# Modulation gates as four rows of 128 with one-hot columns, in a bank that the down projection leaves alone

## The chip, the cores and the metric

The kernel runs on one core of a Trainium2 chip. The metric is the device time of one execution in microseconds, the median of several runs. TensorE (PE in the profile) multiplies, with weights loaded by its own load row (PEld); VectorE is DVE, ScalarE is ACT, GpSimd is POOL, and SyncE (SP) issues most transfers.

## The reference

The program is a chain of transformer blocks over 256 tokens of width 1024. What the change touches is small: in the second block each of two layers takes a modulation from a condition vector, and its gates scale what a mixer or a feed-forward network adds.

```python
cond = silu(c)
for i in range(2):
    mod = cond @ ada_w[i] + ada_b[i]              # 1024 -> 6 * 1024
    sh_m, sc_m, g_m, sh_f, sc_f, g_f = split(mod, 6)
    u = x * (1.0 + sc_m) + sh_m
    x = layer_norm(alpha * x + (1.0 + g_m) * mixer(u), ...)
    u = x * (1.0 + sc_f) + sh_f
    x = layer_norm(alpha * x + (1.0 + g_f) * ffn(u), ...)
```

The feed-forward networks of the first block, `0.5 * (silu(x @ wg) * (x @ wu)) @ wd` with 2816 hidden columns, don't depend on it. The kernel computes the modulation beside them.

## The kernel before, in words

The stages run one after the other: ffn0, ln0, mix0, ln1, ffn1, ln2, ffn2, ln3, mix1, ln4, ffn3, ln5, mlstm, ..., ffn4, ..., s5, ..., moe. A feed-forward pass (ffn0 to ffn3, and ffn4) streams its weights in 33 halves of 1 MB through a ring in SBUF. Halves 0 to 21 (`UP_HALVES` is 22) are the gate and up projections of six chunks of hidden columns (`NC` is 6; five of 512 and one of 256), halves 22 to 32 the down projection, two blocks of 128 hidden rows each. Each half is split into a high part (ScalarE's cast, `upper_act`, L1206) and a low part (VectorE's subtraction, `lower_dve`, L1212), and three products make up for a full float32 one: L967 and L968 (`two`) with the high weights, then L1000 (up) or L1113 (down) with the low weights, for which PE waits until VectorE has made them. Four banks of PSUM (of 8, 512 float32 each) hold a chunk's gate and up sums for two tiles of 128 tokens; the down projection accumulates into banks 4 to 7. Chunk 4 uses banks 4 to 7 and chunk 5 banks 0 to 3.

The modulation is 24 pieces of 512 values, six in each of the passes ffn0 to ffn3. For a piece:

- GpSimd loads 2 MB of `ada_w` in two parts (`load_ada`, L1380), each when VectorE has finished with the part before.
- VectorE multiplies and sums over eight blocks of rows into `ada_acc`, 128 x 512 (`ada`, L1348 and L1350, 16 instructions); what is left is a sum over the 128 partitions.
- PE makes that sum (`mod(c)`, L1134 to L1147) in plain float32. For shift and scale pieces it makes columns (L1146). For gate pieces it makes one row of 512: a column of ones against `ada_acc` (L1142), and then a one-hot column against the eight rows of biases in `ada_gb` (L1143) to add the bias.
- VectorE finishes it (`mod_out`, L1357 to L1371): L1366 adds 1.0 to the row and writes it to a row in SBUF, `gate_row` on partition 0 of `lnp[:, 2]`, two places in turn. `mod_ready` counts the finished pieces.
- GpSimd stores a gate row to `gate_dram` (L1395); from ln6 on the rows are read back to all partitions.

The gate pieces are the last two of each pass, c = 4 and c = 5, eight in all. Their place is written out by hand in `MOD_LATE` (L189): piece 4 after half 21, piece 5 after half 23. Piece 4 is written to bank 5 (`r.banks(c, 0)[1]`), which half 22 is to overwrite, so before half 22 PE waits for `mod_ready` of piece 4 (L1163). VectorE's order around it, in `ffn_dve`: at i = 21 the low part of half 23, `mod_out` of piece 4, the product `hidden(5)` (L1281), and the two parts of `ada` for piece 5; at i = 22 the low part of half 24; at i = 23 that of half 25 and `lower_h(5)` (L1289); at i = 24 that of half 26 and `mod_out` of piece 5. At the end of a pass PE waits for `mod_ready` of all its pieces (L1195).

The biases come by four loads in `mix_params_sp` (L576), which SP issues after half 5 of ffn0, ahead of the constants and the loads of the halves that follow.

Of the kernel before, what the change touches and what calls it, by code (L numbers as in the profile page):

```python
# [21 lines left out]
P = 128  # L22
# [163 lines left out]

UP_HALVES = 4 * NC - 2

MOD_LATE = {UP_HALVES - 1: NC - 2, UP_HALVES + 1: NC - 1}  # L189

FFN_HALVES = UP_HALVES + FT // 2

# [18 lines left out]
def program(nc, A, out, const_at, stages, ctx):  # L211
# [35 lines left out]
    qkv_w = sb("qkv_w", [P, 3, ML_T, QKV_BLOCK])  # L247
    gate_w = sb("gate_w", [P, 3 * ML_T, 2 * ML_HEADS])
    gate_b = sb("gate_b", [P, 2 * ML_HEADS])
    ada_gb = sb("ada_gb", [8, CHUNK])  # L250
    over = sb("over", [1, 1], mybir.dt.int32)
    router = sb("router", [P, KD, EXPERTS])
    mod_col = sb("mod_col", [P, DEPTH, 6, KD])
# [41 lines left out]
    half_landed = [sem(f"half_landed{i}") for i in range(SLOTS - 1)]  # L295
    ring_freed = [sem(f"ring_freed{i}") for i in range(SLOTS + 1)]
    x_landed, consts_landed, params_landed = sem("x_landed"), sem("consts_landed"), sem("params_landed")
    params_clear = sem("params_clear")
    mix_params_landed, second_params_landed = sem("mix_params_landed"), sem("second_params_landed")
    param_rows = sem("param_rows")  # L300
    param_cols = sem("param_cols")
# [266 lines left out]
    def mix_params_sp(sp):  # L568

        def load(dst, src):  # L570
            load_param(sp, mix_params_landed, NMIX, dst, src)

        ada_b = A["ada_b_2"].rearrange("l (v r n) -> l v r n", v=6, n=CHUNK)
        for l in range(DEPTH):
            for w in range(2):
                load(ada_gb[4 * l + 2 * w:4 * l + 2 * w + 2, :], ada_b[l, 2 + 3 * w])  # L576
        load(consts[:, P:], A["consts"][:, P:])
        sp.wait_ge(params_clear, 2)
        for i in range(2):
            half = slice(i * HD, (i + 1) * HD)  # L580
            load(w2bd[half, :, half], A["cmp_w2"].rearrange("l v i o -> i (l v) o"))
            load(poolbd[half, :, half], A["pool_w"].rearrange("l (t h) i o -> h i (l t) o", h=2)[i])
        load(gla_wa2[:, :, :], A["gla_wa2"].rearrange("l r n -> r l n"))
        for l in range(DEPTH):
            load(gla_norm[:, l, :], A["gla_norm_g"][l].partition_broadcast(P))
# [24 lines left out]
        pool.memset(poolbd[:, :, :], 0.0).then_inc(params_clear, 1)  # L610

    def start_dve(dve):
        dve.memset(eps[:, 0:1], 4.0 * LN_EPS)
        dve.memset(eps[:, 1:2], LN_EPS)
        dve.memset(eps[:, 3:4], np.pi / 2)
        dve.memset(eps[:, 4:5], ROUND)
        dve.memset(eps[:, 2:3], RMS_EPS).then_inc(param_rows, 1)
# [251 lines left out]
    expert_gate = late_gate[:, :, 1:]  # L869
    route = cv.take(NT, 128)  # L870
    y_low_at = cv.at
    gate_row = lnp[0:1, 2, :].rearrange("p (a n) -> p a n", a=2)
    xh = z_r[:, :, :].rearrange("p t (k n) -> p t k n", k=KD)
    upper = [ring_r[:, 3, 0:HALF], ring_r[:, 3, HALF:], tail_r[:, :]]
    cv = Carve(of=arena_r)
# [61 lines left out]
    def ffn_sp(sp, key, wg, wu, wd, e=None):  # L937
        for i in range(FFN_HALVES):
            kind, c, j = half_of(i)
            if kind == "d":  # L940
                src = rows(wd)[:, c:c + 2, :]
            else:
                c0, w = CHUNKS[c]
                k = slice(j * KD // 2, (j + 1) * KD // 2) if c < NC - 1 else slice(0, KD)
                src = rows(wg if kind == "g" else wu)[:, k, c0:c0 + w]
            load_half(sp, PN[key, i], src, e)
            if (key, i) == (0, 3):
                columns_sp(sp)
            if (key, i) == (0, 5):
                mix_params_sp(sp)  # L950
            if (key, i) == (1, 5):
                second_params_sp(sp)

    def ffn_pe(pe, r):
        key, e, tiles = r.key, r.e, r.tiles
# [177 lines left out]
        def mod(c):  # L1133

            l, a = divmod(r.n * NC + c, 12)
            v, part = divmod(a, 2)
            dst = r.banks(c, 0)[1]
            pe.wait_ge(ada_ready, 2 * (r.n * NC + c + 1))
            pe.wait_ge(mix_params_landed, NMIX[0])
            if v in (2, 5):  # L1140
                row = 4 * l + 2 * (v // 3) + part
                pe.matmul(dst[0:1, :], ones[:, 0:1], ada_acc[:, :], start=True, stop=False)  # L1142
                pe.matmul(dst[0:1, :], ident[0:8, row:row + 1], ada_gb[:, :], start=False, stop=True).then_inc(mod_done, 1)  # L1143
            else:
                for f in range(4):
                    mm = pe.matmul(dst[:, f:f + 1], ada_acc[:, f * P:(f + 1) * P], ones[:, 0:1], start=True, stop=True)  # L1146
# [3 lines left out]
        for i in range(FFN_HALVES):  # L1150
# [8 lines left out]
            if i >= UP_HALVES:  # L1159
                c = (i - UP_HALVES) // 2  # L1160
                pe.wait_ge(hL_ready, r.groups(max(c, NC - 2)) if tiles == NT and c < NC - 1 else r.groups(c))
                if i == UP_HALVES and has_mod:
                    pe.wait_ge(mod_ready, r.n * NC + NC - 1)  # L1163
            if r.n == 0 and i == 0:
                pe.wait_ge(xl_ready, 4)
            if i == 4 and r.n == 0:
# [101 lines left out]
    def ffn_dve(dve, step, r):  # L1268
# [25 lines left out]
        for i in range(FFN_HALVES):  # L1294
# [13 lines left out]
            if i - 1 in GATE_END and GATE_END[i - 1] > 0 or i == UP_HALVES + 1:  # L1308
# [1 line left out]
                if i != UP_HALVES - 1 or r.e is not None:  # L1310
                    lower_h(c)
                if has_mod and c < NC - 2:
                    mod_out(dve, r.n, c, r.banks(c, 0)[1])
            if has_mod and i - 1 in MOD_LATE and MOD_LATE[i - 1] == NC - 1:
                mod_out(dve, r.n, NC - 1, r.banks(NC - 1, 0)[1])
            if i in UP_END:
                if has_mod and i in MOD_LATE:
                    mod_out(dve, r.n, MOD_LATE[i], r.banks(MOD_LATE[i], 0)[1])
                hidden(UP_END[i])
                if has_mod:  # L1320
                    ada(dve, step, r.n, UP_END[i], 0)
# [35 lines left out]
    def mod_out(dve, n, c, sums):  # L1357
# [3 lines left out]
        dve.wait_ge(mod_done, i + 1)  # L1361
        if v in (2, 5):
            j = 2 * (2 * l + v // 3) + part
            if j >= 2:
                dve.wait_ge(gate_stored, 16 * (j - 1))
            dve.tensor_scalar(gate_row[0:1, j % 2, :], sums[0:1, :], 1.0, None, ALU.add).then_inc(mod_ready, 1)  # L1366
        else:
            bias = cols_b[:, l * 48 + a * 4:l * 48 + a * 4 + 4]

# [12 lines left out]
    def gate_pool(pool, n):  # L1382

        for c in range(NC):
# [7 lines left out]
            if v in (2, 5):  # L1392
                j = 2 * (2 * l + v // 3) + part
                pool.wait_ge(mod_ready, i + 1)
                pool.dma_start(gate_dram[j // 2:j // 2 + 1, part * CHUNK:(part + 1) * CHUNK],  # L1395
                               gate_row[0:1, j % 2, :]).then_inc(gate_stored, 16)

# [2381 lines left out]
```

## Time and profile before

| | us |
|---|---|
| median of 3 runs | 2440.84 (2438.94 to 2440.87) |
| the profiled execution's own time | 2445.78 |
| its span | 2443.9 |
| PE busy | 2367.3 (97%) |
| DVE busy | 1794.0 (73%) |
| ACT busy | 1288.5 (53%) |
| DMA, mean | 244 GB/s |

All durations below are from the profiled execution. Its own time is 1.9 us more than its span and 4.9 us more than the median. A PE row gives when a matmul started and a modelled end; as matmuls are pipelined, the distance between starts is what one costs. A float32 matmul leaves two rows, a weight load each; the products of the passes leave one. "issue" is a wait that the profile puts down to nothing that it shows, such as a wait on a semaphore whose event isn't matched.

### The profile page before, as it was taken

The page shows a single profiled execution, that of the slowest core. Times are in us where ns is not written, and L with a number is a line of the kernel's source. Part 1 is how long each engine was busy: PE and PEld are TensorE (multiplying, and loading weights), DVE is VectorE, ACT ScalarE, POOL GpSimd, SP SyncE. Part 2 cuts the span into 40 slices and gives each one's busy share as a digit, 9 for nine tenths or more (in the row PEclk, how much of TensorE's full clock was granted, in tenths as well). Part 3 has the DMA queues.
Part 4 walks back from the last instruction along what each step waited for, and adds up shares of the span by engine and source line. Part 5 has one row for each costly group of instructions (what it writes and reads, how often), then busy time and mean ns, then how long its engine had stood idle before and what let it go on. Part 6 is the DMA issues. An engine that isn't in the chain of part 4 may idle for free.

```text
span 2443.9 us, 32821 instructions
## 1 busy us (share of the span) xinstructions
PE 2367.3 (97%) x12923; PEld 1953.7 (80%) x12923; DVE 1794.0 (73%) x1996; ACT 1288.5 (53%) x1362; POOL 161.0 (7%) x193
## 2 busy tenths in 40 slices
PE   8999999999999999999999998899999999999997
PEld 7878878878878878879977886677888888888875
DVE  5873377857763468859586557768889899898988
ACT  4332344434432444334454445746778778777774
POOL 0000000000000000000010002600000000000010
PEclk9999899999999999999999998899999999999998
DMA  9767258758757167654225563147999999999995
GB/s 352 256 243 166 78 154 282 272 185 279 270 201 177 53 223 267 245 195 159 104 102 183 184 204 113 49 151 274 380 365 384 378 375 380 377 382 378 373 376 199
DMA packets 306306, 596.81 MB, mean 244 GB/s; under 512 B 61759, under 2 KB 97285, under 8 KB 306061
## 3 DMA queue, kind: packets, MB, share of 16 engines
q1 hardware_dynamic: 285970, 521.09, 60.9%
q0 software_dynamic: 19792, 73.95, 8.9%
q8 instruction: 82, 1.34, 0.2%
q14 instruction: 34, 0.28, 0.0%
q10 hardware_dynamic: 428, 0.15, 0.0%
HBM read 589.36 MB, written 5.78 MB: 244 GB/s over the span
## 4 chain that ended last, share of the span: by engine, by line
PE 88%; DVE 6%; ACT 2%; DMA 2%; issue 1%; ACTq 0%; POOL 0%; DVEq 0%; SPq 0%
PE psum L967 18%; PE psum L968 18%; PE psum L1000 12%; PE psum L1113 6%; PE psum L1513 3%; PE psum L1016 3%; PE psum L1520 2%; PE psum L1130 2%; PE psum L3115 2%; PE psum L960 1%; PE psum L962 1%; PE psum L961 1%; PE psum L2223 1%; DVE ring_r L1212 1%; PE psum L2224 1%
## 5 line engine op out<-in xcount | busy, mean ns | idle before, releaser
L1212 DVE TENSOR_TENSOR ring_r<-ring,ring_r 128x2048 fp32r<-128x2048 f32 x286 | 652.7, 2289 | 200.8 <-ACT ring_r L1206 200.2
L1206 ACT CAST ring_r<-ring 128x2048 fp32r<-128x2048 f32 x286 | 546.5, 1912 | 422.2 <-PE psum L1000 191.6
L1212 DVE TENSOR_TENSOR ring_r<-ring,tail_r 128x2048 fp32r<-128x2048 f32 x143 | 327.4, 2290 | 101.7 <-ACT tail_r L1206 101.4
L1206 ACT CAST tail_r<-ring 128x2048 fp32r<-128x2048 f32 x143 | 273.4, 1912 | 148.4 <-PE psum L1000 69.0
L967 PE MATMUL psum<-ring_r,arena_r 128*128 128x512 f32 (+1 forms) x872 | 337.0, 389 | 6.7 <-issue 4.6
L968 PE MATMUL psum<-ring_r,arena_r 128*128 128x512 f32 (+1 forms) x872 | 332.4, 384 | 0.0
L967 PE MATMUL psum<-ring_r,xT_r 128*128 128x512 f32 (+1 forms) x576 | 214.6, 378 | 2.9 <-ACT ring_r L1206 2.9
L968 PE MATMUL psum<-ring_r,z_r 128*128 128x512 f32 (+1 forms) x576 | 212.7, 375 | 0.0
L967 PEld LDWEIGHTS psum<-ring_r,arena_r 128*128 128x128 f32 x872 | 165.0, 189 | 45.4 <-issue 11.7
L1000 PE MATMUL psum<-ring_r,z_r 128*128 128x512 f32 (+1 forms) x864 | 194.8, 370 | 0.0
L968 PEld LDWEIGHTS psum<-ring_r,arena_r 128*128 128x128 f32 x872 | 165.2, 189 | 30.9
L967 PE MATMUL psum<-tail_r,arena_r 128*128 128x512 f32 (+1 forms) x472 | 176.9, 380 | 2.0 <-DVE arena_r L1289 1.0
L968 PE MATMUL psum<-tail_r,arena_r 128*128 128x512 f32 (+1 forms) x472 | 174.9, 376 | 0.0
L1000 PEld LDWEIGHTS psum<-ring_r,z_r 128*128 128x128 f32 x864 | 152.1, 189 | 27.4
L1000 PE MATMUL psum<-ring_r,arena_r 128*128 128x512 f32 (+1 forms) x704 | 172.7, 371 | 0.6 <-DVE ring_r L1212 0.6
L1350 DVE SCALAR_TENSOR_TENSOR arena<-arena,cond 128x256 f32<-128x256 f32 x336 | 163.0, 485 | 12.0
L1113 PE MATMUL psum<-ring_r,arena_r 128*128 128x512 f32 x640 | 164.9, 390 | 0.3 <-DVE ring_r L1212 0.3
L1000 PEld LDWEIGHTS psum<-ring_r,arena_r 128*128 128x128 f32 x704 | 124.3, 188 | 24.8 <-DVE ring_r L1212 2.1
L1113 PEld LDWEIGHTS psum<-ring_r,arena_r 128*128 128x128 f32 x640 | 120.0, 188 | 25.9 <-DVE ring_r L1212 0.7
L967 PEld LDWEIGHTS psum<-ring_r,xT_r 128*128 128x128 f32 x576 | 108.5, 188 | 22.2 <-DVE xT_r L699 3.1
L968 PEld LDWEIGHTS psum<-ring_r,z_r 128*128 128x128 f32 x576 | 108.5, 188 | 19.0
L1234 ACT ACTIVATE arena<-psum 128x512 f32<-128x512 f32 (+1 forms) x108 | 57.4, 560 | 112.6 <-PE psum L1000 111.7
(566 smaller groups left out, 3835.4 us busy)
## 6 DMA issues: line engine op xcount, KB each, us to landing
ring<-in_moe_w SPq DMA_DIRECT2D x264, 1024.0 KB, 7.3
arena<-in_ada_w POOLq DMA_DIRECT2D x48, 1024.0 KB, 9.9
ring<-in_ffn_wg SPq DMA_DIRECT2D x44, 1024.0 KB, 7.6
ring<-in_ffn_wu SPq DMA_DIRECT2D x44, 1024.0 KB, 7.8
ring<-in_ffn_wd SPq DMA_DIRECT2D x44, 1024.0 KB, 7.0
ring<-in_ffn_w SPq DMA_DIRECT2D x33, 1024.0 KB, 6.4
ring<-in_mlstm_w_in SPq DMA_DIRECT2D x8, 2048.0 KB, 8.1
ring<-in_s_w_glu SPq DMA_DIRECT2D x4, 2048.0 KB, 10.8
```

Source lines behind the costliest of these rows:

```text
L967: pe.matmul(dst, lhs_low, rhs, start=start, stop=False)
L968: return pe.matmul(dst, lhs, rhs, start=False, stop=False)
L1000: mm = pe.matmul(dst, r.x_parts(k0 + k, t)[0], low[:, k, :], start=False, stop=k0 + k == KD - 1)
L1016: mm = pe.matmul(dst, r.x_parts(4 * (i % 2) + k, t)[x_part], w_[:, k, :], start=start and n == 0, stop=stop and n == len(pairs) - 1)
L1113: mm = pe.matmul(acc(t, half), r.h_parts(f, t)[0], low[:, f - f0, half * CHUNK:(half + 1) * CHUNK], start=False, stop=False)
L1130: mm = pe.transpose(r.banks(c, t)[0][:, f * P:(f + 1) * P], h[:, g % 2, f * P:(f + 1) * P], ident)
L1206: act.copy(upper[i % UPPERS], place(PN[r.key, i])).then_inc(upper_ready, 1)
L1212: dve.tensor_tensor(low, raw, upper[i % UPPERS], ALU.subtract).then_inc(lower_ready, 1)
L1234: act.activation(act_g[:, g % 2, 0:w], r.banks(c, t)[0][:, 0:w], ACT.Silu).then_inc(act_ready, 1)
L1350: ins = dve.scalar_tensor_tensor(sums, src, cond[:, k:k + 1], sums, ALU.mult, ALU.add)
L1513: mm = pe.matmul(dst, panel(pn[i], KD, w)[:, k, first:first + m], xT[:, k, :], start=k == 0, stop=k == KD - 1)
L1520: mm = pe.matmul(dst, xT[:, k, t * P:(t + 1) * P], panel(pn[i], KD, w)[:, k, first:first + m], start=k == 0, stop=k == KD - 1)
```

## The change

It (1) makes a gate piece as four rows of 128 on partitions 0 to 3: four matmuls whose weights are four columns cut from a 7-column tile, all zero but for its fourth column, so that block f goes to row f; (2) takes the bias out of PE: the biases are loaded straight into the place of the results, `gate_rows` on four partitions with eight places, and VectorE adds sum, 1.0 and bias there in one instruction; (3) writes both late pieces to bank 3, columns 256 to 511, which chunk 5 (256 columns wide) doesn't use; (4) drops PE's wait before half 22; (5) moves piece 5 to after half 25, and with it its `mod_out` to i = 26. VectorE's wait for an earlier store is gone, as each piece has its own place. Each of the four loads of biases has eight runs of 128 values instead of two of 512, each of the eight stores four instead of one.

```diff
@@ -186,7 +186,7 @@
 
 UP_HALVES = 4 * NC - 2
 
-MOD_LATE = {UP_HALVES - 1: NC - 2, UP_HALVES + 1: NC - 1}
+MOD_LATE = {UP_HALVES - 1: NC - 2, UP_HALVES + 3: NC - 1}
 
 FFN_HALVES = UP_HALVES + FT // 2
 
@@ -247,7 +247,7 @@
     qkv_w = sb("qkv_w", [P, 3, ML_T, QKV_BLOCK])
     gate_w = sb("gate_w", [P, 3 * ML_T, 2 * ML_HEADS])
     gate_b = sb("gate_b", [P, 2 * ML_HEADS])
-    ada_gb = sb("ada_gb", [8, CHUNK])
+    one_row = sb("one_row", [P, 7])
     over = sb("over", [1, 1], mybir.dt.int32)
     router = sb("router", [P, KD, EXPERTS])
     mod_col = sb("mod_col", [P, DEPTH, 6, KD])
@@ -295,7 +295,7 @@
     half_landed = [sem(f"half_landed{i}") for i in range(SLOTS - 1)]
     ring_freed = [sem(f"ring_freed{i}") for i in range(SLOTS + 1)]
     x_landed, consts_landed, params_landed = sem("x_landed"), sem("consts_landed"), sem("params_landed")
-    params_clear = sem("params_clear")
+    params_clear, row_clear = sem("params_clear"), sem("row_clear")
     mix_params_landed, second_params_landed = sem("mix_params_landed"), sem("second_params_landed")
     param_rows = sem("param_rows")
     param_cols = sem("param_cols")
@@ -570,10 +570,10 @@
         def load(dst, src):
             load_param(sp, mix_params_landed, NMIX, dst, src)
 
-        ada_b = A["ada_b_2"].rearrange("l (v r n) -> l v r n", v=6, n=CHUNK)
+        ada_b = A["ada_b_2"].rearrange("l (v r f n) -> l v f r n", v=6, f=4, n=P)
         for l in range(DEPTH):
             for w in range(2):
-                load(ada_gb[4 * l + 2 * w:4 * l + 2 * w + 2, :], ada_b[l, 2 + 3 * w])
+                load(gate_rows[:, 4 * l + 2 * w:4 * l + 2 * w + 2, :], ada_b[l, 2 + 3 * w])
         load(consts[:, P:], A["consts"][:, P:])
         sp.wait_ge(params_clear, 2)
         for i in range(2):
@@ -610,6 +610,9 @@
         pool.memset(poolbd[:, :, :], 0.0).then_inc(params_clear, 1)
 
     def start_dve(dve):
+        dve.memset(one_row[:, :], 0.0).then_inc(row_clear, 1)
+        dve.wait_ge(row_clear, 1)
+        dve.memset(one_row[:, 3:4], 1.0)
         dve.memset(eps[:, 0:1], 4.0 * LN_EPS)
         dve.memset(eps[:, 1:2], LN_EPS)
         dve.memset(eps[:, 3:4], np.pi / 2)
@@ -869,7 +872,7 @@
     expert_gate = late_gate[:, :, 1:]
     route = cv.take(NT, 128)
     y_low_at = cv.at
-    gate_row = lnp[0:1, 2, :].rearrange("p (a n) -> p a n", a=2)
+    gate_rows = lnp[0:4, 2, :].rearrange("p (a n) -> p a n", a=8)
     xh = z_r[:, :, :].rearrange("p t (k n) -> p t k n", k=KD)
     upper = [ring_r[:, 3, 0:HALF], ring_r[:, 3, HALF:], tail_r[:, :]]
     cv = Carve(of=arena_r)
@@ -950,6 +953,12 @@
                 mix_params_sp(sp)
             if (key, i) == (1, 5):
                 second_params_sp(sp)
+
+    def mod_sums(r, c):
+
+        if c >= NC - 2:
+            return r.banks(NC - 1, 1)[1][:, (c - NC + 4) * P:(c - NC + 5) * P]
+        return r.banks(c, 0)[1]
 
     def ffn_pe(pe, r):
         key, e, tiles = r.key, r.e, r.tiles
@@ -1134,13 +1143,14 @@
 
             l, a = divmod(r.n * NC + c, 12)
             v, part = divmod(a, 2)
-            dst = r.banks(c, 0)[1]
+            dst = mod_sums(r, c)
             pe.wait_ge(ada_ready, 2 * (r.n * NC + c + 1))
             pe.wait_ge(mix_params_landed, NMIX[0])
             if v in (2, 5):
-                row = 4 * l + 2 * (v // 3) + part
-                pe.matmul(dst[0:1, :], ones[:, 0:1], ada_acc[:, :], start=True, stop=False)
-                pe.matmul(dst[0:1, :], ident[0:8, row:row + 1], ada_gb[:, :], start=False, stop=True).then_inc(mod_done, 1)
+                pe.wait_ge(param_rows, 1)
+                for f in range(4):
+                    mm = pe.matmul(dst[0:4, :], one_row[:, 3 - f:7 - f], ada_acc[:, f * P:(f + 1) * P], start=f == 0, stop=f == 3)
+                mm.then_inc(mod_done, 1)
             else:
                 for f in range(4):
                     mm = pe.matmul(dst[:, f:f + 1], ada_acc[:, f * P:(f + 1) * P], ones[:, 0:1], start=True, stop=True)
@@ -1159,8 +1169,6 @@
             if i >= UP_HALVES:
                 c = (i - UP_HALVES) // 2
                 pe.wait_ge(hL_ready, r.groups(max(c, NC - 2)) if tiles == NT and c < NC - 1 else r.groups(c))
-                if i == UP_HALVES and has_mod:
-                    pe.wait_ge(mod_ready, r.n * NC + NC - 1)
             if r.n == 0 and i == 0:
                 pe.wait_ge(xl_ready, 4)
             if i == 4 and r.n == 0:
@@ -1310,12 +1318,12 @@
                 if i != UP_HALVES - 1 or r.e is not None:
                     lower_h(c)
                 if has_mod and c < NC - 2:
-                    mod_out(dve, r.n, c, r.banks(c, 0)[1])
+                    mod_out(dve, r.n, c, mod_sums(r, c))
             if has_mod and i - 1 in MOD_LATE and MOD_LATE[i - 1] == NC - 1:
-                mod_out(dve, r.n, NC - 1, r.banks(NC - 1, 0)[1])
+                mod_out(dve, r.n, NC - 1, mod_sums(r, NC - 1))
             if i in UP_END:
                 if has_mod and i in MOD_LATE:
-                    mod_out(dve, r.n, MOD_LATE[i], r.banks(MOD_LATE[i], 0)[1])
+                    mod_out(dve, r.n, MOD_LATE[i], mod_sums(r, MOD_LATE[i]))
                 hidden(UP_END[i])
                 if has_mod:
                     ada(dve, step, r.n, UP_END[i], 0)
@@ -1361,9 +1369,10 @@
         dve.wait_ge(mod_done, i + 1)
         if v in (2, 5):
             j = 2 * (2 * l + v // 3) + part
-            if j >= 2:
-                dve.wait_ge(gate_stored, 16 * (j - 1))
-            dve.tensor_scalar(gate_row[0:1, j % 2, :], sums[0:1, :], 1.0, None, ALU.add).then_inc(mod_ready, 1)
+            if j == 0:
+                dve.wait_ge(mix_params_landed, NMIX[0])
+            dve.scalar_tensor_tensor(gate_rows[:, j, :], sums[0:4, :], 1.0, gate_rows[:, j, :], ALU.add, ALU.add)\
+               .then_inc(mod_ready, 1)
         else:
             bias = cols_b[:, l * 48 + a * 4:l * 48 + a * 4 + 4]
 
@@ -1392,8 +1401,8 @@
             if v in (2, 5):
                 j = 2 * (2 * l + v // 3) + part
                 pool.wait_ge(mod_ready, i + 1)
-                pool.dma_start(gate_dram[j // 2:j // 2 + 1, part * CHUNK:(part + 1) * CHUNK],
-                               gate_row[0:1, j % 2, :]).then_inc(gate_stored, 16)
+                pool.dma_start(gate_dram[j // 2, part * CHUNK:(part + 1) * CHUNK].rearrange("(f n) -> f n", n=P),
+                               gate_rows[:, j, :]).then_inc(gate_stored, 16)
```

## Rows read from the trace of the kernel before

**Rows 1.** The page: part 4, the chain that ended last, by engine.

```profile
PE 88%; DVE 6%; ACT 2%; DMA 2%; issue 1%; ACTq 0%; POOL 0%; DVEq 0%; SPq 0%
```

**Rows 2.** Waits, PE, 0 to 1200 us: waiting line, what ended it, us, times, longest.

```profile
PE psum L967 <- issue: 4.6, 4, 1.2
```

**Rows 3.** Timeline of ffn0 around half 22: start us, us, engine, line.

```profile
143.60 2.08 PE L1000 MATMUL psum<-ring_r,z_r 128*128 128x256 f32 x16
145.60 1.02 PE L1142 MATMUL psum<-arena,consts 128*1 128x512 f32 x2
145.76 2.29 DVE L1212 TENSOR_TENSOR ring_r<-ring,tail_r 128x2048 fp32r<-128x2048 f32 x1
146.55 0.08 PEld L1143 LDWEIGHTS psum<-ada_gb,consts 8*1 8x1 f32 x2 [0.86 <-issue]
146.55 1.01 PE L1143 MATMUL psum<-ada_gb,consts 8*1 8x512 f32 x2
147.95 0.67 DVE L1366 TENSOR_SCALAR lnp<-psum 1x512 f32<-1x512 f32 x1
148.73 0.47 PE L967 MATMUL psum<-ring_r,arena_r 128*128 128x512 f32 x1 [1.16 <-issue]
```

**Rows 4.** Windows: stretch, its us, busy of PE, PEld, DVE, ACT, POOL, PEclk, DMA, GB/s.

```profile
145.60:148.70 3.10, 1.97 (x5) 0.17 (x5) 3.10 (x4) 1.90 (x1) 0.00 (x0) 1.00 1.03 379
148.70:154.58 5.88, 5.85 (x28) 4.89 (x28) 4.33 (x10) 0.07 (x1) 0.54 (x1) 1.00 1.00 365
160.27:162.16 1.89, 1.89 (x5) 0.16 (x4) 1.89 (x2) 1.73 (x1) 0.00 (x0) 1.00 0.35 46
1023.40:1026.52 3.12, 1.96 (x5) 0.19 (x5) 3.12 (x4) 1.90 (x1) 0.00 (x0) 1.00 1.03 378
1026.52:1033.94 7.42, 7.42 (x27) 5.92 (x28) 5.22 (x13) 0.00 (x1) 0.52 (x1) 0.77 0.81 294
1039.70:1041.60 1.90, 1.90 (x6) 0.17 (x5) 1.90 (x2) 1.74 (x1) 0.00 (x0) 1.00 0.48 71
```

**Rows 5.** Timeline, PE, start of mix0: float32 matmuls with 16 weight columns.

```profile
220.86 3.41 PE L1513 MATMUL psum<-xT,ring 128*16 128x256 f32 x15 [0.73 <-ACT xT L669]
```

**Rows 6.** Line L1370, DVE: ns min, median, max of a small addition out of PSUM.

```profile
L1370 DVE SCALAR_TENSOR_TENSOR mod_col<-psum,cols_b x16: 151/153/157, 60.4 to 1004.8; 128x4 f32<-128x4 f32 x16
```

**Rows 7.** Timelines of ffn0 and ffn1 around half 24, and DVE later in ffn0.

```profile
158.64 4.49 DVE L1212 TENSOR_TENSOR ring_r<-ring,ring_r 128x2048 fp32r<-128x2048 f32 x2
...
165.94 1.98 PE L1113 MATMUL psum<-ring_r,arena_r 128*128 128x512 f32 x8
...
180.84 2.29 DVE L1212 TENSOR_TENSOR ring_r<-ring,tail_r 128x2048 fp32r<-128x2048 f32 x1 [3.15 <-ACT tail_r L1206]
...
496.25 0.35 DVE L1348 TENSOR_SCALAR arena<-arena,cond 128x256 f32<-128x256 f32 x1 [2.28 <-DMA arena<-in_ada_w]
...
500.16 4.49 DVE L1212 TENSOR_TENSOR ring_r<-ring,ring_r 128x2048 fp32r<-128x2048 f32 x2
...
500.83 1.02 PE L1142 MATMUL psum<-arena,consts 128*1 128x512 f32 x2
```

**Rows 8.** Chain in order of time, ffn1, half 24: start us, us, what.

```profile
502.80 0.43 PE psum L967
...
506.67 1.81 PE psum L1113 x8
```

**Rows 9.** SP's and ScalarE's issues of transfers: start us, us (first of them a line's).

```profile
L536 ACTq DMA_DIRECT2D arena<-in_c x1: 579/579/579, 1.2 to 1.2; - x1
...
13.17 1.89 SPq L536 DMA_DIRECT2D ada_gb<-in_ada_b x4
...
21.71 6.84 SPq L536 DMA_DIRECT2D gla_wa<-in_gla_wa x1
```

**Rows 10.** The chain, ffn0: the longest transfer in it.

```profile
31.80 23.18 DMA ring<-in_ffn_wg
```

**Rows 11.** SP's waits before issuing loads of halves: us, times, longest.

```profile
SPq L523 <- PE psum L1000: 870.5, 164, 15.0
```

## The prediction

> **What bounds the kernel now.** I read the chain of work that ended last first: PE has 88% of it [rows 1], so what counts is time on PE, either work or waiting. Then PE's waits in the first 1200 us, which hold the four passes with modulation: the longest entry is one that the profile calls issue, four times, 1.2 us each, before line L967 [rows 2]. Four is the number of passes with gate pieces. The timeline of ffn0 shows where it sits [rows 3]. Half 21 ends with sixteen matmuls of L1000; at 145.60 the gate piece's first matmul starts (L1142, two rows), at 146.55 the second (L1143), and half 22 starts only at 148.73. The 1.16 us of idle time before it is the wait of L1163: VectorE is in the low part of half 23 from 145.76 until 145.76 + 2.29 = 148.05, takes the gate row right behind it (L1366, 0.67, until 148.62), and PE starts 0.1 us later. The windows show the same stretch in the first and the last pass, 3.10 and 3.12 us, and the stretch of the second late piece, which has no wait behind it, 1.89 and 1.90 us [rows 4]; the other two passes lie between. So each pass spends 3.12 + 1.90 = 5.0 us of the critical engine on two gate pieces, 20.1 us in all.
>
> **The matmuls.** Now a gate piece is two float32 matmuls of 512 columns, 146.55 - 145.60 = 0.95 us from start to start. In that, the second one's weight load (0.08) begins with its matmul and isn't hidden [rows 3]. After, it is four matmuls of 128 columns: the same 512 columns once, not twice. No row shows four weight columns against 128. Without any exposed load, 512 columns cost 0.95 - 0.08 = 0.87 us. The nearest row is L1513 in mix0, float32, 16 weight columns against 256: 15 rows in 3.41 us, 0.227 each with the last one's modelled tail among them, so its loads are hidden [rows 5]. Half the columns make 0.114 per row, eight rows 0.91 us. The other bound lets every matmul pay an exposed load, as L1143 does: 0.87 + 4 x 0.09 = 1.23 us. I take 0.95, the eight rows and a little for the change of operand, since L1513 is nearest in kind (many small float32 matmuls on the same rows of the array).
>
> The Trainium skill, page "TensorE: Matmul & The Clock Gate", Part 3, states that a weight load overlaps with a running matmul only when it goes to another group of rows; here all four loads go to all rows. By that rule the sum would be that of the first rival. L1513's row speaks against the rule.
>
> **Piece 4, after half 21.** 3.12 becomes 0.95: a gain of 2.17 a pass, with both bounds 1.89 to 2.25. That takes the wait as gone whole. What half 22 needs besides: its weights' high part (ready long before) and the lowered columns of chunk 4, which VectorE finishes just before it turns to L1212 at 145.76 [rows 3]; PE comes at 145.60 + 0.95 = 146.55. Nothing is late there. VectorE still takes the piece only at 148.05, but nobody waits for it then but VectorE itself, and `hidden(5)` behind it is needed only after half 22, which has some 3.67 + 1.81 = 5.5 us of work [rows 8], so at about 152.
>
> **Piece 5.** 1.90 becomes 0.95: a gain of 0.95, bounds 0.67 to 1.03. Its place moves behind half 25. There `ada_acc` is complete (in ffn1, the latest, at 500.16, while half 25 ends near 509, two halves of some 5.5 us after 498.7), so the waits in front of it cost nothing; behind it on PE is only half 26. Its `mod_out` moves two halves, to a stretch in which VectorE idles 3.15 us before each low part [rows 7]; the only one that needs it is PE at the end of the pass.
>
> **VectorE's instruction.** 0.67 for 1 x 512 [rows 3] becomes 4 x 128 with one more operand. Bounds: 0.15 (128 x 4, L1370) [rows 6] and 0.67; I take 0.3, nearer the few columns. It saves 8 x 0.4 us on VectorE and nothing on the path, once PE no longer waits for it. If that cover were gone it would be worth 1.5 us over four passes.
>
> **What is late next.** PE is now 2.17 us earlier at half 24, and VectorE isn't: the second part of `ada` starts when its transfer lands (ffn1: 496.25, after 2.28 idle), and half 24's low part follows, 500.16 + 4.49 / 2 = 502.41 [rows 7]. PE would start half 24 at 500.83 - 2.17 = 498.66 and want the low part after its sixteen high products, 506.67 - 502.80 = 3.87, less the 0.2 by which the first of them (0.43) is slow behind a piece, makes 3.67 [rows 8]: at 502.33. So ffn1 loses about 0.1, with the signal 0.2. In ffn0 the low part is there at 158.64 + 2.25 = 160.89 [rows 7], and PE wants it at 160.27 - 2.17 + 3.67 = 161.77; no loss. The other two have `ada` end earlier against PE than ffn1.
>
> **The rest.** The two memsets and the wait at VectorE's start (about 0.1 us) lie before its first real work, which waits for x; nothing. PE's wait for `param_rows` is for something done in the first microsecond; nothing. The stores (GpSimd) are read from ln6 on; nothing. The four bias loads take SP 1.89 us now, ahead of loads in a stretch where the chain itself is a transfer of 23.18 us [rows 9, 10]. Each gets eight runs of 512 B. ScalarE's load of `c`, also eight such runs, took 0.58 to issue, against 0.25 to 1.0 for one of the four now: between a gain of 0.3 and a loss of 0.4 us; taken as nothing. The far bound is the last rival.
>
> **The sum.** 4 x (2.17 + 0.95) = 12.5, less 0.2: **12.3 us**. The profiled execution took 2445.78, so it would take 2433.5; the median stands 4.9 below it, and I carry the difference over: 2440.84 - 12.3 = **2428.5**. Nothing later takes it back as I read it: SP's loads of halves wait for PE to free places (164 times behind L1000 alone) [rows 11], so the streams of the later stages start earlier with PE.
>
> **The rivals.**
> - **Weight loads are exposed.** A piece costs 1.23, the gain is 4 x (1.89 + 0.67) - 0.2 = 10.0: 2430.8. For it the unhidden load at L1143; against it L1513. Chance 0.17.
> - **A dip of the clock goes too.** After the stall of ffn3 the granted clock is 0.77 in the next stretch, which takes 7.42 us against 5.88 for the same work in ffn0 at 1.00 [rows 4]: 1.54 us. TensorE fell from 2.4 to 1.2 GHz for a while behind 3.1 us of one-column matmuls and idling. One pass of four shows it; without the stall it may not come. Then 13.8: 2427.0. Against it as a term of the sum: the dips lie elsewhere in each execution, and the median already has fewer of them, perhaps. Chance 0.22. The same page, Part 1, says that activity releases the throttle; by that the dip would go.
> - **VectorE takes over at half 24** in all four passes, because `ada_w` lands later against PE when PE runs ahead: piece 5's gain is lost, 8.5 left: 2432.3. Chance 0.06.
> - **Half 22 still waits** for something I took as early (the change doesn't do what it says). Only the matmuls remain, 8 x 0.95 = 7.6: 2433.2. Chance 0.05.
> - **A later transfer holds the end**, the gain is idled away: 2440.8. Transfers have 2% of the chain [rows 1], and the largest piece of it (23.18 us) lies in ffn0, ahead of the change [rows 10]; the other streams follow PE. Chance 0.06.
> - **Slower, by SP's queue in ffn0.** The load of `gla_wa`, with runs of 512 B, held SP for 6.84 us [rows 9]. If all four bias loads did so, 4 x 6.84 - 1.89 = 25.5 us would stand in front of the loads on which the chain hangs [rows 10]: 13.2 slower, 2454.0. It decides from (12.3 + 4.9 + 1.9) / 4 = 4.8 us a load. Against it: ScalarE's load of the same shape took 0.58; `gla_wa` came behind the constants, the largest of these loads. Chance 0.04.
>
> **How the numbers follow.** The forecast has 0.40. Lowest: a piece at 0.87 and the dip gone, 13.1 + 1.5 - 0.2 = 14.4, with a us of scatter: 2425. Highest: the fourth rival, 2433. That leaves out little more than the last two, 0.10, and tails. A measurement of this kernel tells 0.2%, 4.9 us, from no change. All cases but the last two are faster by more: 0.90; within it 0.06; slower 0.04.
>
> **What would show it.** In the trace after: no issue wait of 1.2 before L967 in the four passes; the stretch from the piece's first matmul to half 22 about 0.95 us (1.23: the first rival); eight rows about 0.11 apart; `mod_out` near 0.3; half 24's L1113 waiting for L1212 only in ffn1; SP's bias loads under 1 us each; SP's first loads of ffn0's halves unmoved. I am wrong if the passes are each shorter by 3.1 us and the end isn't earlier by 12, or if a new wait stands before turn(5) or half 24.

## The result, and the profile after

| | before | after |
|---|---|---|
| median, us | 2440.56 (2438.94 to 2440.87, 4 runs) | 2422.14 (2418.18 to 2423.74, 4 runs) |
| profiled execution: time, span, us | 2445.78, 2443.9 | 2422.41, 2420.6 |
| mean granted clock of PE | 0.978 | 0.982 |

The ratio is 0.9923 (0.9911 to 0.9935): 18.4 us or 0.77% faster. The forecast was 2428.5 with a range from 2425: right in sign, 6.4 us too little, and the median lies below the range.

The page after, parts 1 and 4 (the chain by engine): as in [rows 1] PE has nearly all of the chain, 89%.

```profile
PE 2348.6 (97%) x12955; PEld 1948.6 (81%) x12955; DVE 1790.0 (74%) x1998; ACT 1287.8 (53%) x1362; POOL 163.0 (7%) x193
...
PE 89%; DVE 6%; ACT 2%; issue 1%; DMA 1%; POOL 0%; ACTq 0%; DVEq 0%; SPq 0%
```

The timeline of after in ffn0, around both late pieces (start us, us, engine, line), answers to [rows 3]:

```profile
144.08 1.04 PE L1152 MATMUL psum<-arena,one_row 128*4 128x128 f32 x8
...
144.25 2.28 DVE L1220 TENSOR_TENSOR ring_r<-ring,tail_r 128x2048 fp32r<-128x2048 f32 x1
...
145.05 0.50 PE L976 MATMUL psum<-ring_r,arena_r 128*128 128x512 f32 x1
...
146.44 0.27 DVE L1374 SCALAR_TENSOR_TENSOR lnp<-psum,lnp 4x128 f32<-4x128 f32 x1
146.65 0.73 DVE L1289 TENSOR_TENSOR arena<-arena,psum 128x256 f32<-128x256 f32 x2
...
167.52 1.04 PE L1152 MATMUL psum<-arena,one_row 128*4 128x128 f32 x8
...
168.49 0.50 PE L976 MATMUL psum<-tail_r,arena_r 128*128 128x512 f32 x1
```

Half 22 starts 145.05 - 144.08 = 0.97 us after the piece's first matmul, where it took 3.12; the same distance is 168.49 - 167.52 = 0.97 at the second piece, where it was 1.90 [rows 4]. VectorE takes the piece at 146.44, 1.4 us after half 22 began, and nobody waits.

The windows of after over the two pieces (stretch, its us, busy of PE, PEld, DVE, ACT, POOL, PEclk, DMA, GB/s) answer to [rows 4]: PE is busy throughout.

```profile
144.08:145.05 0.97, 0.97 (x10) 0.61 (x9) 0.97 (x2) 0.81 (x1) 0.00 (x0) 1.00 1.04 431
167.52:168.56 1.04, 1.04 (x10) 0.68 (x9) 0.00 (x0) 0.87 (x1) 0.00 (x0) 1.00 0.00 0
```

PE's waits of after up to 1200 us (line, what ended it, us, times, longest): the entry of [rows 2] has no successor.

```profile
PE psum L2232 <- ACT tail_r L2192: 4.0, 1, 4.0
PE psum L630 <- DMA consts<-in_consts: 2.9, 1, 2.9
PE psum L976 <- ACT ring_r L1214: 2.7, 1, 2.7
```

So far all is as forecast, and so are the passes. The stages can be cut where GpSimd issues a layer norm's load; ffn0 counts from the start, moe from the last such load to the end. GpSimd's timeline of after, start of ffn1, its end, start and end of ffn3 (the two rows of before behind it):

```profile
355.49 0.60 POOL L737 DMA_DIRECT2D lnp<-in_ln_g  x1 [117.75 <-DVE x L782]
550.67 0.57 POOL L737 DMA_DIRECT2D lnp<-in_ln_g  x1 [41.74 <-DVE x L782]
...
888.25 0.59 POOL L737 DMA_DIRECT2D lnp<-in_ln_g  x1 [119.32 <-DVE x L782]
1081.41 0.57 POOL L737 DMA_DIRECT2D lnp<-in_ln_mix_g  x1 [39.73 <-DVE x L804]
```
```profile
361.58 0.60 POOL L734 DMA_DIRECT2D lnp<-in_ln_g  x1 [119.29 <-DVE x L779]
559.78 0.58 POOL L734 DMA_DIRECT2D lnp<-in_ln_g  x1 [50.88 <-DVE x L779]
```

ffn1 took 559.78 - 361.58 = 198.20 and takes 550.67 - 355.49 = 195.18. Cut in this way, in us:

| kernel | ffn0 | ffn1 | ffn2 | ffn3 | moe | span |
|---|---|---|---|---|---|---|
| before | 218.2 | 198.2 | 197.2 | 197.8 | 804.7 | 2443.9 |
| after | 213.6 | 195.2 | 194.2 | 193.2 | 797.8 | 2420.6 |
| null_before | 215.4 | 198.2 | 197.2 | 197.8 | 798.5 | 2433.5 |
| null_after | 213.0 | 195.2 | 194.2 | 193.2 | 801.4 | 2422.1 |
| look_before | 215.3 | 199.8 | 197.2 | 197.8 | 800.6 | 2437.8 |
| look_before2 | 217.6 | 199.8 | 197.2 | 197.8 | 801.4 | 2439.9 |
| look_after | 212.1 | 195.2 | 194.2 | 193.2 | 798.2 | 2419.4 |
| wait_back | 212.2 | 196.9 | 195.9 | 194.9 | 795.1 | 2417.0 |
| early5 | 212.8 | 196.0 | 194.2 | 194.2 | 799.1 | 2422.5 |
| padded | 215.4 | 198.2 | 197.2 | 196.2 | 796.2 | 2429.2 |
| fill_stall | 217.8 | 198.3 | 197.3 | 196.3 | 800.2 | 2439.4 |
| shift32_after | 212.7 | 195.9 | 194.1 | 193.8 | 801.4 | 2425.7 |
| look_align1 | 215.3 | 199.8 | 197.2 | 197.8 | 795.1 | 2432.4 |

ffn1 and ffn2 lost 3.02 and 3.04 us, where the forecast had 3.12 - 0.2 and 3.12. Four times that is 12.1 of the 18.4 us between the medians; 6 us have no place yet. The two profiled executions differ by more, 23.3 us: beyond their 3.0 each, ffn0 and ffn3 are 1.5 shorter each, moe 6.9 and the stretch before moe 2.8, and the other stretches 1.7 longer in all. Neither moe nor the stretch before it has a gate piece.

### The profile page after: what moved, and what is told of

Read it like the earlier page. It is cut to its first block, busy times and chain, and to the rows that moved or that the text cites. A ratio compares the mean times of both kernels' runs of the same rounds, so it can differ in the third digit from the quotient of the medians.

```text
span 2420.6 us, 32882 instructions
## 1 busy us (share of the span) xinstructions
PE 2348.6 (97%) x12955; PEld 1948.6 (81%) x12955; DVE 1790.0 (74%) x1998; ACT 1287.8 (53%) x1362; POOL 163.0 (7%) x193
## 4 chain that ended last, share of the span: by engine, by line
PE 89%; DVE 6%; ACT 2%; issue 1%; DMA 1%; POOL 0%; ACTq 0%; DVEq 0%; SPq 0%
PE psum L976 19%; PE psum L977 19%; PE psum L1009 13%; PE psum L1122 5%; PE psum L1522 3%; PE psum L1025 3%; PE psum L1529 2%; PE psum L1139 2%; PE psum L3124 2%; PE psum L969 1%; PE psum L971 1%; PE psum L970 1%; DVE ring_r L1220 1%; PE psum L2342 1%; PE psum L2232 1%; PE psum L2233 1%
## 5 line engine op out<-in xcount | busy, mean ns | idle before, releaser
L1220 DVE TENSOR_TENSOR ring_r<-ring,ring_r 128x2048 fp32r<-128x2048 f32 x286 | 652.2, 2289 | 189.0 <-ACT ring_r L1214 188.8
L1214 ACT CAST ring_r<-ring 128x2048 fp32r<-128x2048 f32 x286 | 546.6, 1912 | 400.7 <-PE psum L1009 212.8
L1220 DVE TENSOR_TENSOR ring_r<-ring,tail_r 128x2048 fp32r<-128x2048 f32 x143 | 327.3, 2289 | 99.4 <-ACT tail_r L1214 99.3
L1122 PE MATMUL psum<-ring_r,arena_r 128*128 128x512 f32 x640 | 164.8, 389 | 0.3 <-DVE ring_r L1220 0.3
L1122 PEld LDWEIGHTS psum<-ring_r,arena_r 128*128 128x128 f32 x640 | 120.0, 188 | 25.9 <-DVE ring_r L1220 0.7
```

The costliest lines, as they stand in the source:

```text
L1122: mm = pe.matmul(acc(t, half), r.h_parts(f, t)[0], low[:, f - f0, half * CHUNK:(half + 1) * CHUNK], start=False, stop=False)
L1214: act.copy(upper[i % UPPERS], place(PN[r.key, i])).then_inc(upper_ready, 1)
L1220: dve.tensor_tensor(low, raw, upper[i % UPPERS], ALU.subtract).then_inc(lower_ready, 1)
```

## The experiments

The ratios are to the kernel before, run beside each on the same chip, with a 95% interval. The forecast's account explains 12 of 18 us. Theories for the rest: dips of the clock (stretches in which the granted clock of PE falls from 1.00, 2.4 GHz, to 0.50, 1.2 GHz) that end with the stall; something that streams the weights faster; the new loads; or mere scatter between chips and executions.

**null_before, null_after**: both kernels once more, unedited.

> The kernel before, unchanged. The profile of before was of an execution 4.9 us longer than the median. Theory A (each place of the change gave what was forecast, some 3.05 us a pass, 12.2 in all, and what is over, some 6 us in the medians and 11 in the profiled executions, lies in dips of the granted clock and in the start, which differ from one execution to the next and from one kernel to the next): ratio 1.000, but this profile's stages differ from the first profile's by 1 to 3 us in ffn0, mix0, mix1, s5 and moe, and not at all in ffn1 and ffn2. Theory B (the change gives something more in a later stage, by itself): this profile's stages agree with the first one's within 0.5 us, moe (804.7 us) among them.

> The kernel after, unchanged. Both theories: ratio near 0.9925 again (18 us less). Theory A: its moe lies anywhere between 797 and 805 us and ffn1 at 195.2; theory B: moe at 797.8 within 0.5 us again.

0.9995 (0.9986 to 1.0004) and 0.9920 (0.9907 to 0.9934). The gain is real: 19.5 us here. moe of one and the same kernel scatters by 6 us between single executions (table: before's 798.5 to 804.7, after's 797.8 to 801.4), so a single trace can't say where 3 us of moe are, and only medians of whole executions tell whether they are there. Single executions of both kernels (**look_before**, **look_before2**, **look_after**) gave 2439.66, 2441.74 and 2421.23 us and serve the table and the count of dips below.

> The kernel before once more, for its trace: a third look at where the dips lie. Theory A: a dip of 1.5 us behind the stall of ffn3 a third time (197.8 us), ffn1 198.2 and ffn2 197.2 without. Theory C, or chance: it may lie in another pass or in none.

> The kernel before, a fourth trace: moe 798 to 805; one or two dips of 1.5 us behind the stalls of the four passes.

> The kernel after, a third trace: ffn1 195.2, ffn2 194.2, ffn3 193.2, no dip in any pass behind the late pieces, moe 795 to 801.

**wait_back**: after, with PE's wait before half 22 again.

```diff
+                if i == UP_HALVES and has_mod:
+                    pe.wait_ge(mod_ready, r.n * NC + NC - 1)
```

> After with PE's wait for piece 4 before half 22 put back. PE would start half 22 when VectorE, which is at the low part of half 23 until then, has made the piece: about 1.8 us later in each of four passes, 7.3 us slower than after. Theory A with dips caused by the stall: up to 6 us more on top, as the dips come back with the stall (ratio to before 0.998 to 0.9955). Theory B, dips by chance: 0.9955 and ffn1 197.0 us, with no clock dip behind the stall.

0.9941 (0.9927 to 0.9954). Its timeline in ffn0 and its entry in PE's waits up to 1200 us:

```profile
140.94 1.04 PE L1152 MATMUL psum<-arena,one_row 128*4 128x128 f32 x8
...
141.10 2.28 DVE L1222 TENSOR_TENSOR ring_r<-ring,tail_r 128x2048 fp32r<-128x2048 f32 x1
143.30 0.27 DVE L1376 SCALAR_TENSOR_TENSOR lnp<-psum,lnp 4x128 f32<-4x128 f32 x1
...
143.68 0.47 PE L976 MATMUL psum<-ring_r,arena_r 128*128 128x512 f32 x1 [1.70 <-issue]
```
```profile
PE psum L976 <- issue: 6.8, 4, 1.7
```

ffn1 to ffn3 are longer by 1.7 us each, four waits make 6.8, and the ratios differ from null_after's by 0.0021, 5.1 us, with intervals of 3 us to either side. So the trace confirms that the wait, and VectorE's low part ahead of `mod_out`, is what the forecast took it for; the ratio agrees with it, but is too coarse to size it.

**early5**: after, with piece 5 behind half 23 again.

```diff
-MOD_LATE = {UP_HALVES - 1: NC - 2, UP_HALVES + 3: NC - 1}
+MOD_LATE = {UP_HALVES - 1: NC - 2, UP_HALVES + 1: NC - 1}
```

> After with piece 5 back at its old place behind half 23. Forecast's reading: its new place gives nothing, as its data is ready in time at the old one too except in ffn1, where ada ends at 500.2 against a half 23 that now ends near 498.7: 1.5 us slower in ffn1, and some tenths in ffn2 and ffn3, so 2 us slower than after in all. Rival: no difference.

0.9935 (0.9921 to 0.9948). ffn1 and ffn3 grow by 0.9 and 1.0 us, ffn2 by nothing; PE's waits up to 1200 us name it:

```profile
PE psum L1152 <- DVE arena L1358: 1.8, 2, 1.0
```

With half 22 early, PE reaches the old place before VectorE has finished `ada_acc`. Expected were 1.5 us in ffn1 and some tenths in the other two. The later place is not indifferent: by this trace it guards 1.9 us of the gain, and the ratio, 0.0015 above null_after's, is within its interval of that.

**padded**: after, with 3.0 us of dense float32 matmuls behind piece 5 in each pass, whose results nobody reads: ffn1 and ffn2 are as long as before, but without the idle time and the one-column matmuls.

```diff
                 mod(MOD_LATE[i])
+                if i == UP_HALVES + 3:
+                    for n in (512, 512, 512, 256):
+                        pe.matmul(r.banks(NC - 1, 0)[1][:, 0:n], ones, const("bands")[:, 0:n], start=True, stop=True)
```

> After, with PE doing dense extra matmuls behind piece 5 in each pass (128 weight columns, 512 + 512 + 512 + 256 columns in float32, 3.0 us, into a bank that nobody reads): the passes are as long as before, but without idle time and one-column matmuls. What is asked: where the 5 us come from by which the executions of after lose less to clock dips than those of before (mean granted clock 0.982 against 0.980). Theory A (the dips of before hang on the stall and the thin matmuls of the late pieces): clock 0.982 as after, time after + 12.1 = 2433 to 2434, ratio 0.997. Theory C (dips elsewhere depend on when the stages come, and the shorter passes moved them): clock back near 0.980, ratio 0.999 to 1.000.

0.9970 (0.9959 to 0.9981), 12 us above null_after: 4 x 3.0 us of PE's time cost 12 us, so time on PE in these passes is worth its own length and no more. And 0.3% or 7 us stay gained in a kernel whose passes are as long as before. That part isn't in the pieces.

**fill_stall**: before, with dense matmuls of 512 and 256 columns in PE's idle 1.16 us, results not read.

```diff
                 if i == UP_HALVES and has_mod:
+                    for n in (512, 256):
+                        pe.matmul(acc(0, 0)[:, 0:n], ones, const("bands")[:, 0:n], start=True, stop=True)
                     pe.wait_ge(mod_ready, r.n * NC + NC - 1)
```

> Before, with PE doing dense extra matmuls of 1.3 us (128 weight columns, 512 + 256 columns in float32) in the time in which it waits for piece 4; the time of the passes stays within 0.2 us each. Theory A: no dip behind the stall of ffn3 (ffn3 196.2 instead of 197.8) and clock 0.9805 or more, ratio 0.998 to 0.9993. Theory C: ffn3 and the clock as before, ratio 1.000.

0.9988 (0.9979 to 0.9997), 2.9 us faster for doing more work, with an interval from 0.7 to 5.1. The windows over half 22 of ffn3, in look_before (before again, one execution) and in fill_stall:

```profile
1021.93:1029.93 8.00, 6.84 (x23) 5.06 (x22) 6.20 (x13) 0.62 (x1) 0.52 (x1) 0.79 0.97 352
```
```profile
1024.57:1032.57 8.00, 8.00 (x35) 5.95 (x34) 6.00 (x12) 1.02 (x2) 0.52 (x1) 1.00 0.94 341
```

Granted clock 0.79 against 1.00, and ffn3 is 197.8 against 196.3. Such a dip, 1.5 to 1.7 us, stood behind the stall in 11 of 28 passes of seven executions that have both the stall and the one-column matmuls (before, null_before, look_before, look_before2, loads_only, align_before, look_align1), and in none of 48 passes of twelve executions that lack at least one of the two (three of after, fill_stall, early5, padded, and the three shift and three arena kernels below). In windows of 1 us the granted clock of a dip is 0.50 for about 3 us, the level of 1.2 GHz. 11 x 1.55 / 7 = 2.4 us per execution. wait_back, with 1.0 us of thin matmuls and 1.7 idle, has no dip in its four passes, too few to say which of the two brings it.

**loads_only**: before, with only the bias loads in the new form. The kernel leaves out the right biases: its bias matmul reads four of the new rows, so the gates carry other values, and only its time is of use.

```diff
-                load(ada_gb[4 * l + 2 * w:4 * l + 2 * w + 2, :], ada_b[l, 2 + 3 * w])
+                load(bias_rows[:, 4 * l + 2 * w:4 * l + 2 * w + 2, :], ada_b[l, 2 + 3 * w])
```

> Before, with the four bias loads in the new form alone (eight runs of 128 values on four partitions each; the bias matmul reads four of these rows, so the gates have other biases). ffn0 net of dips was 4.3 us shorter after than before, 1.3 more than ffn1 and ffn2. Theory D (the new loads help the transfer-bound start): ffn0 1.3 us shorter than before, ratio 0.9995. Rival (the start differs from one execution to the next): ffn0 net of dips anywhere between 213.5 and 216.5, ratio 1.000.

0.9999 (0.9990 to 1.0008), nothing. Left over, then, are some 4 to 5 us (18.4 or 19.5, less 12.1 and 2.4) that belong neither to passes nor to dips. What else the edit does: `ada_gb` is 2048 bytes of each partition, `one_row` takes 32, and every tile behind moves down by 2016. The ring starts at byte 65248 of a partition before, 224 beyond a multiple of 256, and at 63232 = 247 x 256 after; the arena moves likewise from 155360 to 153344 = 599 x 256. The DMA lines (part 6) end with the median us from issue to landing; after:

```profile
ring<-in_moe_w SPq DMA_DIRECT2D x264, 1024.0 KB, 7.0
arena<-in_ada_w POOLq DMA_DIRECT2D x48, 1024.0 KB, 8.7
```

Before they were 7.3 and 9.9. (By this measure every trace with an aligned ring has 6.8 to 7.1 for `in_moe_w`, every other one 7.3.) The next runs move nothing but tiles.

**align_before** (and again as **look_align1**): before, with 32 bytes more ahead of the ring, which puts ring and arena on multiples of 256.

```diff
     row_of_token = sb("row_of_token", [P, 2, NT], U32)
+    spare = sb("spare", [P, 8])
```

> Before, with 32 unused bytes per partition allocated ahead of the ring, nothing else. In before the ring begins at byte 65248 of its partition, 32 short of a multiple of 256; after took a tile of 2048 B away and put one of 28 B in its place, and the ring came to 63232, a multiple of 256. Theory E (the weights' transfers run better into an aligned ring, and this is the gain that the forecast lacks): the loads of moe land in a median of 7.0 us instead of 7.3, ScalarE waits for them some 18 us instead of 38, ffn0's first 30 us move 367 GB/s instead of 350, ratio 0.9978 (5 to 6 us less), stall dips as in before. Rival (it is the shorter passes that changed moe and ffn0): 7.3 us, 350 GB/s, ratio 1.000.

> Before with the ring moved to a multiple of 256, once more, for its stages. Its first trace had ffn0 215.3 and moe 801.1, no shorter than before's other traces, while its timed runs were 5 us faster. If the gain lies in moe, as between after and shifted after (797.9 against 802.4 on the mean), moe is now near 797; if it lies nowhere in particular but in the number of clock dips, 799 to 802.

0.9979 (0.9968 to 0.9989), and again 0.9979 (0.9969 to 0.9989): 5.1 us for 32 bytes. The transfers show it. Windows over the first 30 us, before, align_before and shift32_after (below); the last column is GB/s:

```profile
0.00:30.00 30.00, 24.18 (x117) 20.67 (x118) 14.34 (x15) 16.30 (x19) 4.24 (x10) 1.00 0.97 349
```
```profile
0.00:30.00 30.00, 24.43 (x108) 20.86 (x109) 14.31 (x15) 15.11 (x13) 4.25 (x10) 0.94 0.97 367
```
```profile
0.00:30.00 30.00, 23.88 (x108) 20.18 (x109) 14.33 (x17) 15.12 (x13) 4.24 (x10) 0.94 0.97 352
```

At the same busy share of the queues, an aligned ring takes 367 GB/s, the others 349 and 352; over all the traces it is 362 to 368 against 349 to 353. The engines that read the ring don't explain it: ScalarE's cast of 2048 columns takes 1912 ns and VectorE's subtraction 2289 and 2288 ns on the mean, in before and in align_before. How the faster landings become 5 us isn't shown in full. The mean granted clock of the 22 timed executions of this kernel is 0.9812, that of the 38 of before beside them 0.9804; by that, as an estimate, some 2 of the 5.1 us may come as fewer dips in later stages.

**shift32_after, shift64_after, shift128_after**: after, with the same tile of 32, 64 or 128 bytes, which takes ring and arena off their multiple.

> After, with 32 unused bytes ahead of the ring (63264, 32 past a multiple of 256). Theory E: the loads of moe land in 7.3 us again, ffn0 1.3 us and moe 3 us longer, ratio 0.994 to 0.9945: 2427, which is the forecast of 2428.5 less the 2 us of stall dips. Rival: as after, 0.992.

> After, with 64 unused bytes ahead of the ring (63296: a multiple of 64, not of 128 or 256). If a boundary of 64 bytes is what counts, as after (7.0 us, 0.992); if one of 128 or 256, as shifted by 32 bytes (7.3 us, 0.994).

> After, with 128 unused bytes ahead of the ring (63360: a multiple of 128, not of 256). If 64 or 128 bytes count, as after (7.0 us); if 256, 7.3 us.

0.9948 (0.9934 to 0.9961), 0.9942 (0.9927 to 0.9957) and 0.9949 (0.9933 to 0.9965): all three give back 5 to 7 us of after's gain, and 64 or 128 bytes are no better than 32. moe's loads land in 7.3 again; ffn1 and ffn3 are 0.7 to 0.8 longer, and moe is 802.4 on the mean of three traces against 799.1 of after's three, within its scatter. ScalarE's waits for the moe loads (us, times, longest), after and then shift32_after:

```profile
ACT ring_r L1214 <- DMA ring<-in_moe_w: 16.0, 13, 4.1
ACT tail_r L1214 <- DMA ring<-in_moe_w: 3.2, 4, 2.1
```
```profile
ACT ring_r L1215 <- DMA ring<-in_moe_w: 28.5, 29, 3.2
ACT tail_r L1215 <- DMA ring<-in_moe_w: 6.3, 11, 1.0
```

Before had 29.7 and 9.6. This goes with the layout in most executions, though not in each: align_before's showed 30.0 and 12.5, look_align1's, the same kernel, 7.9 and 3.8. So where in moe the us are gained these traces don't show.

The Trainium skill, page "DMA: Bandwidth & Descriptors", section "How a descriptor splits into AXI transactions", says that a transaction can read less than 256 bytes but must start at a multiple of 256, so that a descriptor with another start fetches bytes that it doesn't use. Direction and unit agree (7.3 against 7.0 us; 128 no better than 32), though here it is the destination in SBUF that is moved, of which the section says nothing; no run here shows that the same rule is at work.

**arena_off, arena_off64, arena_off256**: after, with a gap of 32, 64 or 256 bytes between ring and arena, so that the ring stays aligned.

```diff
-    places = (... ("z", [P, NT, D]), ("arena", [P, ARENA]))
+    places = (... ("z", [P, NT, D]), ("gap", [P, 8]), ("arena", [P, ARENA]))
```

> After, with 32 unused bytes between z and the arena: the ring stays at 63232, a multiple of 256, the arena with the places of ada_w goes to 153376, 32 past one. If the ring's place makes the 6 us by which the shifted kernels are slower than after, 0.992 as after, moe near 798, the weights' loads of moe in 7.0 us; if the arena's does, 0.9945, with ffn1 and ffn3 0.7 us longer (195.9 and 193.9). Likeliest: both, each in its own stages: ffn1 and ffn3 0.7 longer, moe as after, ratio 0.9925.

> After with 64 unused bytes between z and the arena instead of 32. With 32 every product that takes its weights from the arena and its moving operand from the ring went from 0.2266 to 0.234 us from start to start, and the kernel was 22 us slower than after. If PE's two reads disturb each other by their distance within some unit of bytes, 64 gives yet another step: anything between 0.22 (faster than after, ratio under 0.99) and 0.234 (1.001). If it is any distance but a multiple of 256, as with 32: 1.001.

> After with 256 unused bytes between z and the arena: both begin at multiples of 256 as in after, only their distance changes. If distance within 256 bytes is what counts, as after: 0.992, step 0.2266, ffn1 195.2.

1.0016 (1.0005 to 1.0027), 1.0009 (0.9998 to 1.0021) and 0.9918 (0.9892 to 0.9944). 32 bytes cost 23 us (1.0016 against 0.9920), 256 bytes nothing. None of the expectations for arena_off had that: they lay between 0.992 and 0.9945. moe's loads land in 6.9, so it isn't the ring's transfers. The arena's own loads land in 9.4 instead of 8.7, but the shifted kernels have that too (9.8 to 10.0) and lose only 5 to 7 us. It is PE: the chain of arena_off in ffn0 has the first of these lines, that of after the second.

```profile
165.18 1.87 PE psum L1122 x8
```
```profile
165.78 1.81 PE psum L1122 x8
```

Eight products take 1.87 against 1.81 us. Line L1122 by itself (ns min, median, max), in after, arena_off64 and arena_off256:

```profile
L1122 PE MATMUL psum<-ring_r,arena_r x640: 388/389/497, 148.8 to 2396.6; 128*128 128x512 f32 x160
```
```profile
L1122 PE MATMUL psum<-ring_r,arena_r x640: 388/398/496, 145.8 to 2419.4; 128*128 128x512 f32 x160
```
```profile
L1122 PE MATMUL psum<-ring_r,arena_r x640: 388/389/504, 146.1 to 2392.8; 128*128 128x512 f32 x160
```

All 4872 rows of products with one operand in the arena and the other in ring or tail add up to 1640.0 us in after, 1660.1 in arena_off, 1659.9 in arena_off64, 1638.3 in arena_off256 and 1639.1 in shift32_after; the other 8083 have 1712.7 in after and 1714.0 in arena_off. That is 20 of the 23 us. So a product whose weights lie in the arena and whose moving columns lie in the ring takes longer when the distance between the two tiles is 32 or 64 bytes off a multiple of 256. The arena's place alone doesn't do it: in shift32_after it is 32 bytes off too, and the distance is kept. In before and after the distance is such a multiple (90112 = 352 x 256), so this plays no part in the result.

## Why the prediction was right or wrong

- **The piece**: 0.95 forecast, 0.97 measured, twice per pass. Eight rows of L1152 have (1.04 - 0.27) / 7 = 0.110 from start to start, as L1513's halved row said (0.114) [rows 5]. The source view of after (ns min/median/max) gives the loads:

```profile
L1152 PEld LDWEIGHTS psum<-arena,one_row x64: 82/87/87, 144.1 to 1036.9; 128*4 128x4 f32 x64
L1152 PE MATMUL psum<-arena,one_row x64: 272/273/273, 144.1 to 1037.1; 128*4 128x128 f32 x64
```

  87 ns of load would not fit beside a matmul in 0.110 if it were exposed. The first rival falls, and with it, for these matmuls, the rule quoted from the Trainium skill ("TensorE: Matmul & The Clock Gate", Part 3) as it was quoted; the same Part also has loads that target a background weight buffer pulled ahead of running matmuls, which these rows don't contradict. The rival's price was also too low by its own terms: it counted four loads a piece at 0.09 us, and the trace has eight.
- **The wait before half 22** is gone, 2.17 forecast, 3.12 - 0.97 = 2.15 measured; the fourth rival falls. wait_back's trace confirms its cause.
- **Piece 5**: 0.95 forecast, 1.90 - 0.97 = 0.93 measured, nothing new in front. early5 shows that this rests on the new place.
- **`mod_out`**: 0.3 taken, 0.27 measured.
- **Half 24 in ffn1**: 0.1 to 0.2 us of waiting forecast, none in after, but 0.4 in ffn1 of shift32_after. The forecast read VectorE's start there from a landing of `ada_w` at 9.9 us after issue; aligned, it is 8.7.
- **The bias loads** were taken as nothing: loads_only, 0.9999. SP took 2.12 us for the four instead of 1.89. The last rival falls; padded leaves nothing of "a later transfer holds the end".
- **The clock's dips** were kept out of the sum, as a rival at 0.22 and 1.5 us. They come in 11 of 28 passes and were worth about 2.4 us (fill_stall: 2.9), and all are gone in after. Its doubt, that the median has fewer of them than the profiled execution with its one, isn't borne out: seven traced executions hold 1.6 each on the mean.
- **The step that failed** is "The rest": it costs every edit by its instructions, and so puts the two tiles, `ada_gb` out and `one_row` in, at nothing, without a reason. Their difference puts ring and arena on multiples of 256 bytes, and that is worth 5.1 us in before and 5 to 7 in after. In the shifted kernels, which have the whole change but this, the medians are 2427.4 to 2428.4, against the forecast's 2428.5, or 2427.0 with the dips.

The sum in its place: 12.1 (passes) + 5.1 (alignment) + 2.4 (dips) = 19.6, measured 18.4 and 19.5. With the dips in it the forecast would still have been 2427.0; the layout's 5.1 us take it to 2421.9, beside the measured 2422.14. No end of the range had a term for the layout, hence 2425 as its low end. No experiment beats after: arena_off256 (0.9918) is its equal.

What stays open: whether idling or thin matmuls bring the dips; by which waits the faster landings shorten the kernel; and why PE's products slow down with the distance between their two tiles.

## What to carry to other kernels

When a change adds or removes a tile, work out where every tile behind it comes to lie, above all those that transfers write to in bulk; the unchanged schedule with 32 bytes of padding is the control that parts layout from schedule. Here it paid to have the ring of streamed weights on a multiple of 256 bytes of the partition (0.2%), and the tile of the products' weights at a multiple of 256 from it (0.9%); try both. Before pricing a moved step at nothing, ask whether its old place would still be free once the engine runs ahead.

## What was not expected of the hardware

- Loads of 1 MB into SBUF at 32, 64, 128 or 224 bytes beyond a multiple of 256: 7.3 us from issue to landing against 7.0, 349 to 353 GB/s against 362 to 368, 0.2% of this kernel.
- Products of 128 x 128 weights with 512 columns take 1.87 / 8 = 0.234 us against 1.81 / 8 = 0.226 when the distance between their tiles is 32 bytes off such a multiple: 23 us here.
- Behind 3.1 us of one-column matmuls and idling the granted clock dips to 0.50 (1.2 GHz) in 11 of 28 passes, at a cost of some 1.55 us each; with the idle part filled by dense matmuls, in none of 4.
